# Sixteen units of an input projection as eight pairs of seven block products

## What is computed

```
proj = h @ w_in
gq, gk, gv, g_lr, g_gate, hq, hf, hi, h_gate = jnp.split(proj, IN_OFFSETS, axis=-1)
...
forget = lb + (1.0 - lb) * jax.nn.sigmoid(hf.astype(f32))
o_hgrn = chunk_gated_linear_attention(
    split_heads(jax.nn.silu(hq.astype(f32)), HGRN_HEADS),
    split_heads(1.0 - forget, HGRN_HEADS),
    split_heads(hi.astype(f32), HGRN_HEADS),
    split_heads(jnp.log(forget), HGRN_HEADS), CHUNK)
o_hgrn = merge_heads(rms_norm(o_hgrn, hgrn_norm_g)).astype(h.dtype) * jax.nn.silu(h_gate)
return jnp.concatenate([o_gla, o_hgrn], axis=-1) @ w_out
```

## Time and profile before

| what | value |
|---|---|
| median of three runs | 1174.47 us (1173.69 to 1175.45) |
| span of the profiled execution | 1173.7 us |
| PE, DVE, ACT, POOL busy | 98%, 69%, 51%, 38% |
| three H1 groups | 169.70 us, 56.57 each |
| group G | 55.53 us |

### The profile page before, as it was taken

How to read it: one execution, slowest core, us unless ns; L and a number is a source line. 1 busy time by engine, 2 the same in 40 slices (tenths; PEclk the granted TensorE clock), 3 DMA queues, 4 the chain that set the end, 5 groups by cost and what they waited for, 6 DMA issues and landing times.

```text
span 1173.7 us, 15673 instructions
## 1 busy us (share of the span) xinstructions
PE 1154.4 (98%) x5651; PEld 958.1 (82%) x5651; DVE 807.6 (69%) x958; ACT 597.9 (51%) x899; POOL 444.0 (38%) x274
## 2 busy tenths in 40 slices
PE   7999999999999999999999999999999999999997
PEld 6788788888888888888888888888878888888886
DVE  6898766554536358367987755676796784966776
ACT  7763554646464647235655555455663443434325
POOL 1021111111111115326444442435367574666751
PEclk9899999999999999999999999999999999999999
DMA  9765241021111114341455435534723737437203
GB/s 351 261 224 171 90 145 36 18 55 36 36 36 36 37 38 143 90 161 72 117 171 165 158 118 171 179 135 130 220 72 118 251 98 253 151 123 280 92 1 144
DMA packets 148765, 152.02 MB, mean 130 GB/s; under 512 B 6228, under 2 KB 117976, under 8 KB 146008
## 3 DMA queue, kind: packets, MB, share of 16 engines
q1 hardware_dynamic: 148696, 151.12, 39.7%
HBM read 117.02 MB, written 34.08 MB: 129 GB/s over the span
## 4 chain that ended last, share of the span: by engine, by line
PE 91%; DVE 3%; issue 2%; DMA 2%; SPq 1%; ACT 1%; DVEq 0%; ACTq 0%
PE unit_bank L1338 33%; PE unit_bank L1640 8%; PE unit_bank L1642 8%; PE unit_bank L1641 8%; PE small_bank L1642 8%; PE small_bank L1640 8%; PE small_bank L1641 8%; PE small_bank L1338 3%; PE small_bank L1473 2%; DMA ada_slot<-in_w_ada_dram 2%; PE small_bank L1377 1%; PE small_bank L1465 1%; DVE ada_acc L1741 1%; DVE state L1941 1%; DVE op_lo L2254 0%
## 5 line engine op out<-in xcount | busy, mean ns | idle before, releaser
L777 POOL TENSOR_TENSOR wr_lo<-quarter,wr_hi 128x512 fp32r<-128x512 f32 x122 | 196.2, 1622 | 175.0 <-ACT wr_hi L1130 174.9
L1338 PE MATMUL unit_bank<-a_hi,w_hi 128*128 128x512 f32 x560 | 223.7, 400 | 0.0
L1338 PE MATMUL unit_bank<-a_hi,w_lo 128*128 128x512 f32 x560 | 218.7, 391 | 0.0
L1338 PE MATMUL unit_bank<-a_lo,w_hi 128*128 128x512 f32 x560 | 218.5, 390 | 0.0
L721 POOL TENSOR_TENSOR w_lo<-raw,w_hi 128x1024 fp32r<-128x1024 f32 x27 | 67.7, 2506 | 348.5 <-ACT w_hi L832 348.5
L1640 PE MATMUL unit_bank<-op_hi,wr_hi 128*128 128x512 f32 x452 | 176.6, 391 | 0.7 <-DVE op_lo L2254 0.6
L1642 PE MATMUL unit_bank<-op_hi,wr_lo 128*128 128x512 f32 x452 | 176.0, 389 | 0.0
L1641 PE MATMUL unit_bank<-op_lo,wr_hi 128*128 128x512 f32 x452 | 175.9, 389 | 0.0
L1640 PE MATMUL small_bank<-op_hi,wr_hi 128*128 128x512 f32 x448 | 174.6, 390 | 0.0
L1642 PE MATMUL small_bank<-op_hi,wr_lo 128*128 128x512 f32 x448 | 174.4, 389 | 0.0
L1641 PE MATMUL small_bank<-op_lo,wr_hi 128*128 128x512 f32 x448 | 174.4, 389 | 0.0
(11 more groups left out here) (273 smaller groups left out, 1856.3 us busy)
## 6 DMA issues: line engine op xcount, KB each, us to landing
quarter<-in_w_mlp_dram SPq DMA_DIRECT2D x128, 256.0 KB, 4.4
hidden_scratch<-hid SPq DMA_DIRECT2D x98, 256.0 KB, 2.9
ada_slot<-in_w_ada_dram SPq DMA_DIRECT2D x48, 512.0 KB, 5.5
op_full<-hidden_scratch SPq DMA_DIRECT2D x21, 1024.0 KB, 4.9
raw<-in_w_in_dram SPq DMA_DIRECT2D x29, 512.0 KB, 3.8
raw<-in_w_out_dram SPq DMA_DIRECT2D x16, 512.0 KB, 4.0
x_stage<-in_x_dram SPq DMA_DIRECT2D x8, 512.0 KB, 5.1
x_scratch<-xT SPq DMA_DIRECT2D x2, 2048.0 KB, 8.3
```

Source lines behind the costliest of these rows:

```text
L777: pool.tensor_tensor(wr_lo[slot][:, :, :], split_source(n), wr_hi[slot][:, :, :].bitcast(F32), ALU.subtract).then_inc(wr_lo_pool, 1)
L1338: return pe.matmul(out_ap, left, right, start=start, stop=stop)
```

## The change

The four groups behind `H0` (three times `H1`, and `G`: 16 units) become eight **pairs**. A pair is two units taken as 2 x 2 blocks: two unit columns by two halves of the input width, times two halves of the input width by two halves of the tokens. Its results are four quarters "11", "12", "21", "22", each of 128 x 512, in the four banks `unit_bank`, and it takes seven block products of 4 tiles x 3 = 12 matmuls each. Per head the early pair is (HQ, HF) and the late one (GG, HI); in the last group the pairs are (HG+P, HG) and (HG+2P, HG+3P), with P = 128 columns.

- **Input sums.** They are made once. POOL adds high and low parts back together and forms the sums and differences of the four input blocks, in seven instructions of 128 x 2048, in places of 8 KB per partition (`x_sum0` to `x_sum3`) where the residual `xT` lay. `xT` is stored to DRAM before (8 x 512 KB) and read back before the output projection (4 x 1 MB). Of the four sums T1, T4 stay on chip as `t1_hi/t1_lo`, `t4_hi/t4_lo`; T2 replaces the input block (0, half 1) in `a_hi/a_lo`; T3 is stored to DRAM, 2 x 1 MB.
- **The seventh product** (`P7`, with T3) is read from DRAM for each pair, in four pieces: `piece_x` (512 KB) for pieces 0 and 2, `piece_y` (2 x 256 KB) for 1 and 3. It stands on PE in four places between other products.
- **Weights.** A pair's weights come as four `pair_quarter` of 256 KB. DVE forms S3, S2, S1, S4; ACT rounds seven high parts of 128 x 512 (`pair_high`), POOL subtracts seven low parts (`pair_low`). They have four places: P7; P1 and P5; P2 and P4; P6 and P3.
- **Joins.** ACT copies a bank twice per pair (`copy_part`), DVE adds five times (`join`: "11", "u", "22", "21", "12"). The banks rotate: P1 and the quarter "21" of pair p+1 take the bank of "11" of pair p; "11" of p+1 that of "22"; "22" (the seventh product) that of "12"; "12" that of "21".
- **Attention steps** of a head now stand at nine places instead of eight; the values are turned (`v`) in the last. The mixed output of head 0 goes to DRAM and back. The last unit of `H0` takes its halves in the other order.
- The loop is written out, so `misc` memsets and loop branches go. Output projection: the first half takes its tiles in the order 1, 2, 3, 4, 5, 0, 6, 7.

The diff, cut to its core:

```diff
-U_OUT = 29
-U_MLP = 37
+U_OUT = 13
+U_MLP = 21
...
+PAIR_PLACE = {P7: 172, P1: 180, P5: 180, P2: 176, P4: 176, P6: 168, P3: 168}
+JOINS = 5
+QUARTER_JOIN = {"11": 1, "22": 3, "21": 4, "12": 5}
...
-        s[1] += [("up", 0, 0, 2), ("up", 1, 0, 3), ("sc", 0, 0, 1)]
-        s[2] += [("k", 0, 1, 0), ("sc", 0, 1, 1)]
-        s[3] += [("o", 0, 0, 2)]
-        s[4] += [("up", 2, 1, 3), ("up", 3, 1, 0), ("ss", 0, 0, 1)]
-        s[5] += [("o", 0, 1, 2)]
-        s[6] += [("ss", 0, 1, 3)]
+        s[1] += [("up", 0, 0, 2), ("up", 1, 0, 3)]
+        s[2] += [("sc", 0, 0, 1)]
+        s[3] += [("k", 0, 1, 0), ("sc", 0, 1, 1)]
+        s[4] += [("o", 0, 0, 2)]
+        s[5] += [("up", 2, 1, 3), ("up", 3, 1, 0), ("ss", 0, 0, 1)]
+        s[6] += [("o", 0, 1, 2)]
+        s[7] += [("ss", 0, 1, 3)]
...
-            with e.Fori(1, 4) as h:
-                group("H1", h + 2, h)
-            group("G", 6, None)
+            for h in range(1, 4):
+                paired(h + 2, h)
+            gates(6)
...
+                if j == 6:
+                    sp.wait_ge(read["x"], 16)
+                    for m in range(KT):
+                        sp.dma_start(x_dram[:, m, :], xT[:, m, :]).then_inc(x_out, 16)
+                if j == 9:
+                    sp.wait_ge(t_made, T_MADE_0 + 4)
+                    for i, part in enumerate((t3_hi, t3_lo)):
+                        sp.dma_start(t3_dram[:, :, i, :], part[:, :, :].bitcast(F32)).then_inc(t3_stored, 16)
...
+                elif i == 2:
+                    sp.wait_ge(pair_sum, pair_sum_of(p - 1, "S1"))
+                elif i == 3:
+                    sp.wait_ge(pair_sum, pair_sum_of(p - 1, "S1"))
+                    sp.wait_ge(pair_lo, PAIR_LO_0 + split_of(p - 1, P4))
+                else:
+                    sp.wait_ge(pair_sum, pair_sum_of(p - 1, "S4"))
+                    sp.wait_ge(pair_lo, PAIR_LO_0 + split_of(p - 1, P6))
...
+            for p in range(PAIRS):
+                more = p + 1 < PAIRS
+                if more:
+                    load_pair_quarter(p + 1, 2)
+                if p == 3:
+                    sp.wait_ge(gated, 1)
+                    sp.dma_start(mixed_dram, mixed[:, 0, :]).then_inc(mixed_out, 16)
+                load_piece(p, 2)
+                load_piece(p, 3)
+                if more:
+                    load_pair_quarter(p + 1, 3)
+                    load_piece(p + 1, 0)
+                    load_pair_quarter(p + 1, 0)
+                    load_pair_quarter(p + 1, 1)
+                    load_piece(p + 1, 1)
...
+            for u in range(2, 10):
                 low(u, u % 2)
-            with pool.Fori(0, 4) as i:
-                for j in range(4):
-                    low(4 * i + 13 + j, (1 + j) % 2)
-            evens = (0, 2, 4, 6)
-            low_tiles(16, mixed, a_hi, a_lo, 0, evens)
-            low_tiles(24, mixed, a_hi, a_lo, 1, evens)
-            pool.wait_ge(gated, 10)
+            pool.wait_ge(x_out, X_OUT_0 + 16 * KT)
+            pool.wait_ge(lo_dve, 16)
+            add_parts(xs[1], 0, 1, 0)
+            add_parts(xs[0], 1, 1, 1)
+            subtract(xs[3], xs[0], xs[1], 2)
+            low(10, 0)
+            pool.wait_ge(t_high, T_HIGH_0 + 1)
+            pool.tensor_tensor(t3_lo[:, :, :], xs[3][:, :, :], t3_hi[:, :, :].bitcast(F32), ALU.subtract).then_inc(t_made, 1)
+            low(11, 1)
+            pool.wait_ge(t3_stored, T3_STORED_0 + 32)
+            add_parts(xs[2], 0, 0, 4)
+            subtract(xs[1], xs[1], xs[2], 5)
+            low(12, 0)
+            subtract(xs[3], xs[0], xs[1], 6)
+            add_parts(xs[0], 1, 0, 7)
+            subtract(xs[2], xs[0], xs[3], 8)
+            pool.wait_ge(t_high, T_HIGH_0 + 2)
+            pool.tensor_tensor(t1_lo[:, :, :], xs[1][:, :, :], t1_hi[:, :, :].bitcast(F32), ALU.subtract).then_inc(t_made, 1)
+            for p in range(PAIRS):
+                for prod in SPLIT_ORDER:
+                    pair_low(p, prod)
...
+                    pair_high(0, P1)
+                    pair_high(0, P7)
+                    act.wait_ge(unit_filled[1], 13)
+                    act.activation(blocks(a_hi, 0, 1), xs[3][:, :, :], ACT.Copy).then_inc(t_high, 1)
+                    read_out(7)
+                    pair_high(0, P2)
+                    act.wait_ge(t_done, T_DONE_0 + 1)
+                    act.activation(t4_hi[:, :, :], xs[2][:, :, :], ACT.Copy).then_inc(t_high, 1)
                     act.wait_ge(q_cum_ready, gi + 1)
-                    tanh_and_copy(3)
-                next_high(3)
-            groups(act, group)
+                    tanh_and_copy(3, (1, 0))
...
+                pair_high(early, P6)
+                wait_join(act, early, 0)
+                keys(0)
+                copy_part(early, 0)
+                pair_high(early, P5)
+                pair_high(early, P4)
+                copy_part(early, 1)
+                pair_high(early, P3)
+                act.wait_ge(filled["sc"], before("sc", gi) + 1)
+                tanh_of(q_rel, 0, early, "11")
+                pair_high(late, P1)
+                pair_high(late, P7)
+                keys(1)
+                act.wait_ge(gated, h)
+                forget_tanh(1, early, "22")
+                pair_high(late, P2)
+                forget_tanh(0, early, "21")
+                output(0)
+                act.wait_ge(hk_ready, h + 1)
+                act.activation(t0[:, :], t0[:, :], ACT.Ln).then_inc(log_a, 1)
+                act.wait_ge(filled["sc"], before("sc", gi + 1))
+                tanh_of(q_rel, 1, early, "12")
...
+                norm(0)
+                pair_high(late, P4)
+                output(1)
+                copy_part(late, 1)
+                pair_high(late, P3)
+                act.wait_ge(q_rel_ready, gi + 1)
+                tanh_of(t0, 0, late, "11")
+                pair_high(late + 1, P1)
+                norm(1)
+                act.wait_ge(filled["o"], before("o", gi + 1))
+                value_of(1, late, "22")
+                pair_high(late + 1, P7)
+                pair_high(late + 1, P2)
+                value_of(0, late, "21")
+                tanh_of(t0, 1, late, "12")
...
+                    if p == 0:
+                        half, u = {P1: (0, 12), P2: (1, 13), P5: (0, 13)}[prod]
+                        pe.wait_ge(unit_read[half], u)
+                    else:
+                        c = {P1: "11", P2: "22", P5: "21"}[prod]
+                        pe.wait_ge(c_read[c], C_READ_0[c] + p)
...
+            def seventh_piece(p, j):
+                place, dst = PAIR_PLACE[P7], quarter_bank(p, "22")
+                if j == 0:
+                    pe.wait_ge(pair_lo, PAIR_LO_0 + split_of(p, P7))
+                    if p == 0:
+                        pe.wait_ge(unit_read[1], 12)
+                    else:
+                        pe.wait_ge(c_read["12"], C_READ_0["12"] + p)
...
+                pair_product(early, P1)
+                attend(0)
+                seventh_piece(early, 0)
+                pair_product(early, P2)
+                seventh_piece(early, 1)
+                attend(1)
+                pair_product(early, P6)
+                seventh_piece(early, 2)
+                attend(2)
+                pair_product(early, P5)
+                seventh_piece(early, 3)
+                attend(3)
+                pair_product(early, P4)
+                attend(4)
+                pair_product(early, P3)
+                pair_product(late, P1)
+                attend(5)
+                seventh_piece(late, 0)
+                pair_product(late, P2)
+                seventh_piece(late, 1)
+                attend(6)
+                pair_product(late, P6)
+                seventh_piece(late, 2)
+                pair_product(late, P5)
+                seventh_piece(late, 3)
+                attend(7)
+                pair_product(late, P4)
+                pair_product(late, P3)
+                if name == "H1":
+                    attend(8)
...
+                dve.wait_ge(log_a, gi + 1)
+                dve.tensor_tensor_scan(own_cum[:, :], carry[:, :], t0[:, :], 0.0, ALU.mult, ALU.add).then_inc(cum_ready, 1)
+                dve.wait_ge(cum_ready, gi + 1)
+                dve.tensor_tensor(chunked(t0), chunked(own_cum), at_chunk(CH // 2 - 1, own_cum), ALU.subtract).then_inc(d_mid, 1)
+                dve.wait_ge(filled["k"], before("k", gi + 1))
+                wait_join(dve, early, JOINS)
+                dve.tensor_tensor(chunked(k_end), chunked(own_cum), at_chunk(CH - 1, own_cum), ALU.subtract).then_inc(d_last, 1)
+                silu_of(q_rel, 1, early, "12", made + 2)
+                weight_sum_of(late, "S1")
+                dve.wait_ge(e_k, gi + 1)
+                dve.wait_ge(hk_ready, h + 1)
+                dve.tensor_tensor(k_rel[:, :], k_rel[:, :], t1[:, :], ALU.mult).then_inc(k_rel_ready, 1)
+                states(1)
```

725 lines of the change are left out of this document (601 added, 124 removed).

## The result

| | before | after |
|---|---|---|
| median of the runs, us | 1174.5 | 1214.69 (1212.35 to 1216.5) |
| ratio after to before | | 1.0345 (95%: 1.033 to 1.036) |
| profiled span, us | 1173.7 | 1210.6 |

A forecast was written before the change was run, and what follows sets the result against it. The prediction took PE, busy 98% of the span, as the bound. Removing 22.3 us against 19.1 us of new waits turned the 1173.7 us span into 1170.5, a median of 1171.3, with a range of 1161 to 1183.

The forecast's parts named there:

- The row for it: DVE's 128 x 512 a_lo: 0.69 us with POOL quiet, 1.64 beside POOL; the forecast used the quiet value.
- The removed work: Over eight pairs 768 matmuls become 672; 96 fewer at 0.2267 us save 21.8 us of PE.
- Stall 2: Late seventh product in three heads waits for its bank, held by DVE's silu behind the running sum; 2.4 us each, 7.2.
- Stall 1: First pair's P2 after H0 waits for ACT's bank copy behind high parts and rounded copies; 6.1 us.
- term of 1.4 us for a late `t1_hi`: End of H0: POOL's chain delays `t1_hi`, so ACT begins the head's outputs up to 1.4 us later.
- the clock in the stages: One fall of PE's granted clock, behind the 6.1 us wait before pair 0's P2; 1.7 us.
- the output projection: Its first tiles' weights wait for a slot the last pair holds, its last tile for the last gate; 0.5 us.
- stall 3: End of each of three paired heads: value copies on ACT stand behind norm(1); 1.2 us each, 3.6.
- the bound that I had named and not taken: End of a paired head: 2.5 us if the next P1's high part waits for its 256 KB load.
- Rival 3: Short waits at the late seventh product lower the clock and POOL's low parts delay DVE; 1180.0 us, chance 25%.
- two busy sums: Work per paired head: ACT 38.6 and DVE 40.6 us against PE's 51, so neither bounds it by sum.

The follow-up runs named there:

- Run 1: Changed kernel with POOL's eight input sums and two low parts in P1 and H0 replaced by zero fills that read nothing; 1193.89 us, ratio 1.0174.
- run 3: Changed kernel with the early pair's tanh and silu of "12" moved ahead of Ln on ACT and the running sum on DVE; 1223.59 us.
- run 5: Changed kernel, DVE order only: silu of "12" right behind the running sum, second half of the states behind the first difference; 1216.98 us.
- run 6: Changed kernel with both value copies ahead of norm(1) on ACT and the last join ahead of norm(1) on DVE; 1211.95 us.
- run 9: Kernel of run 5 with SP's load of piece 2 ahead of the next pair's third weight quarter; 1217.48 us, ratio 1.0372.
- Run 11: Changed kernel with half of products P4 and P3 of every pair left out, 12 matmuls a pair; 1212.46 us, ratio 1.0333.
- run 10: Changed kernel with POOL's sums in eighths, silu and states moved, piece 2 first, values before norm(1), last H0 banks read first; 1200.98 us.
- run 12: Kernel of run 9 with POOL's sums in quarters and norm(1) last, behind values on ACT and the output gate on DVE; 1192.39 us.

## Why the prediction was wrong

**The step that failed** is the scope of the change in the sum. I priced POOL's ten long instructions only as a chain that makes `t1_hi` late, and asked what they release, not what they hold up while they run. The row for it stood in the rows: 1.64 against 0.69 us for the same DVE instruction beside POOL. I used it for the paired heads, where POOL's instructions are of 1.6 us, and there called it a wait for one POOL instruction. Applied to P1 and H0, with POOL's instructions at 4.8 us, it says that every DVE instruction with two on-chip inputs may last up to 4.8 us more. Two adaLN sums, q_rel and a small addition in P1 and two products in H0 lie on the path. Price: 16.0 us of PE's waits and, around the two long ones, two stretches of lower clock (160.2 to 167.0 and 218.2 to 228.4), 20.9 in P1 and H0, of which 18.3 are left at pair 0. Run 1 takes all of it back. I had put no wait of PE into that stretch, and my range could not hold it. It is 18.3 of the 40.1 us between the forecast span, 1170.5, and the measured 1210.6; the other 21.8 are the terms mis-sized below and what is left untraced.

**What stood.** The removed work: 96 matmuls (5651 and 5555 on the pages); G, which has no running sum, took 50.0 us against 55.36 - 5.44 = 49.9, first matmul to first matmul. Stall 2: 2.4 a head forecast, with 2.1 if POOL holds nothing up; 3.2 measured, 2.14 with the low parts as fills.

Stall 1 agrees partly by luck: 6.1 forecast, 1.74 + 4.16 = 5.9 measured. Its term of 1.4 us for a late `t1_hi` did not occur: ACT had made `t1_hi` at 225.61 and idled until PE released the outputs at 237.09. In its place stands a wait for a weight sum of DVE that I had not counted:

```profile
237.09 0.60 ACT L1243 ACTIVATE stat<-small_bank 128x512 f32<-128x512 f32 x1 [9.58 <-PE small_bank L1889]
...
243.78 0.63 ACT L1336 ACTIVATE pw_hi<-pw_full 128x512 fp32r<-128x512 f32 x1 [2.10 <-DVE pw_full L2583]
```

**What was mis-sized.** By the most: the clock in the stages (6.0 us more than forecast), the output projection (4.9), stall 3 (3.6 over three heads) and stall 2 (2.5). Stall 3 was 1.2 a head and is 2.3 to 2.5. ACT's row before P1's high part of the next pair shows the bound that I had named and not taken, 1.80 us for a quarter load:

```profile
304.61 0.63 ACT L1336 ACTIVATE pw_hi<-pair_quarter 128x512 fp32r<-128x512 f32 x1 [1.80 <-DMA pair_quarter<-in_w_in_dram]
```

The output projection was 0.5 and is 5.4: 0.5 + 2.66 us of waits for the low parts of its weights and one fall of the clock. For the clock I had counted one fall, 1.7. In the stages I find four stretches in which 128 x 512 matmuls start 0.43 us apart, behind waits of 4.16, 3.22, 2.35 and 3.23 us; summed over 0.2267 they cost 1.4, 2.2, 1.6 and 2.5, so 7.7 us. A window with the second of them:

```profile
343.00:355.00 12.00, 9.00 (x40) 7.66 (x40) 10.72 (x17) 9.04 (x10) 4.03 (x3) 0.72 0.43 132
```

Rival 3 had this mechanism (12.0 us at 0.72 granted); I gave it 25%. Its condition, a wait over 1.4 us, is not the whole of it: the first wait of 3.21 us at 7l0 was followed by matmuls at full rate, the second and third, of the same length, were not. The Trainium skill ("TensorE: Matmul & The Clock Gate", Part 1) says that an idle PE falls to half rate, and the trace agrees that waits bring it down, not that every wait of a length does. What tells the waits apart is open.

**Was it a sum of stalls at all?** In the three paired heads it was not. My method found where PE waits and added. That came near the size of some waits, and it misleads on what removing one is worth: runs 3, 5, 6 and 9 each took away one kind of wait, and in heads 2 and 3 PE still idles 4.6 to 7.8 us, at other places. Run 11 takes away 5.4 us of PE's work per head, and PE idles 5.4 and 4.9 us longer. A paired head is bound by the chain of its own vector work, from the forget gate over Ln, running sum, exponentials, states, norms and joins to the values, in the order in which DVE and ACT hold it. I had dismissed that bound with two busy sums, 38.6 and 40.6 us under 51. After, the window of head 2 shows DVE 40.73 and ACT 35.12 busy in 59.26 us:

```profile
312.20:371.46 59.26, 53.68 (x285) 44.52 (x283) 40.73 (x56) 35.12 (x52) 20.83 (x15) 0.94 0.38 116
```

DVE's sum was right, ACT's 3.5 us too high, and both said nothing, since the chain alternates between the two engines and PE. Only runs 10 and 12, which take norm(1) out of the chain ahead of the values and of the next head's first step, cut PE's idle time in heads 2 and 3, to between 3.4 and 4.4 us, and the heads to between 56.2 and 56.9. Within the heads run 12 differs from run 9 by that place alone (norm(1), and with it the value copy ahead of P2's high part). Head 2 of run 9, then of run 12:

```profile
314.69:376.22 61.53, 55.67 (x285) 45.73 (x283) 40.05 (x56) 35.14 (x52) 20.22 (x15) 0.92 0.37 112
```

```profile
298.43:354.69 56.26, 51.82 (x286) 42.46 (x284) 40.54 (x55) 34.93 (x53) 19.59 (x15) 1.00 0.39 122
```

Of the 5.3 us between them only 1.4 are idle time (5.86 and 4.44); 3.9 are PE's busy time, at a granted clock of 0.92 and 1.00. So a good part of the gain came through the clock and not through the chain itself. Which other links make up the idle time that is left is not isolated. Nor is head 1's greater length, beyond stall 1 and its clock.

About 2.4 us of the stages' difference (12.3, against -21.8 removed, 24.0 waits and 7.7 clock) are no wait and no lower clock: the head of run 12 above, at a clock of 1.00, keeps PE busy for 51.82 us, where 56.4 - 5.4 = 51.0 is left of a head before. That is 0.8 a head; why is not traced.

## What to carry to other kernels

When work moves to POOL, price it at the instructions of DVE that run beside it, not at POOL's own idle time: each DVE instruction with two on-chip inputs can wait for one whole POOL instruction that reads, and long POOL instructions on tiles of 8 KB cost most where DVE's are short and on the path. Where the banks have lost their slack, a wait that is removed shows the next link; take work away from the supposed bound once (as run 11) before any tuning of its waits. Compare idle time and granted clock apart, since the length of a stage mixes them. In a stage whose vector chain is as long as PE's work, taking matmuls away only lengthens PE's waits, as in heads 2 and 3 of run 11.

## What the runs showed of the hardware

- A DVE addition of 128 x 4 with both inputs on chip lasted 4.45 us beside a POOL sum of 128 x 2048, 1.24 beside quarters and 0.15 in the kernel before; it counts as busy time in the profile, not as waiting.
- POOL's own sums lasted longer beside DVE's two-input ones: 128 x 2048 took 4.53 us with DVE idle (at 193.95) and 5.61 beside `k_rel` (at 205.46). A quarter took 1.5 to 1.7 us on average and an eighth 1.0.
- A fill of 128 x 2048 by POOL took 1.81 us; DVE's two-input instructions beside it (0.15 us for the 128 x 4 addition) kept their length, and once a one-input tensor_scalar of 128 x 4 lasted 1.57 us instead of 0.17, to the fill's end.
- Three waits of PE of 3.2 us each, at the same place of the program, were followed once by full clock and twice by the lower one.
